# A recurrence of six steps: solved keys copied by two engines, keys turned before the second level's update

## The reference, cut to what matters

```python
kk = jnp.einsum('bhnid,bhnjd->bhnij', k, k)
t_mat = jnp.eye(c) + jnp.where(strict, kk * decay, 0.0) * beta[..., :, None]
u = solve(t_mat, v * beta[..., None])
wk = solve(t_mat, k * (beta * jnp.exp(gam))[..., None])
k_dec = k * jnp.exp(gam[..., -1:] - gam)[..., None]
# per chunk, in order:
w = u_c - jnp.einsum('bhck,bhkv->bhcv', wk_c, s)
s_new = cd_c * s + jnp.einsum('bhck,bhcv->bhkv', kd_c, w)
o = jnp.einsum('bhck,bhkv->bhcv', qd_c, s) + jnp.einsum('bhij,bhjv->bhiv', qk_c, w)
```

## Time and profile before

| what | us |
|---|---|
| median of 3 runs | 2874.38 (2871.8 to 2876.06) |
| profiled execution | 2869.82 |
| its span | 2868.0 |
| PE busy | 2716.9 (95%) |
| DVE busy | 1132.7 (39%) |
| ACT busy | 522.7 (18%) |
| POOL busy | 535.4 (19%) |
| mean granted TensorE clock | 0.975 |

### The profile page before, as it was taken

How to read it: one execution, slowest core, us unless ns; L and a number is a source line. 1 busy time by engine, 2 the same in 40 slices (tenths; PEclk the granted TensorE clock), 3 DMA queues, 4 the chain that set the end, 5 groups by cost and what they waited for, 6 DMA issues and landing times. The chain is left out here.

```text
span 2868.0 us, 35950 instructions
## 1 busy us (share of the span) xinstructions
PE 2716.9 (95%) x15102; PEld 1783.4 (62%) x15102; DVE 1132.7 (39%) x2206; ACT 522.7 (18%) x1160; POOL 535.4 (19%) x371
## 2 busy tenths in 40 slices
PE   7998999999999999999999999789969999996998
PEld 4443467777886446888887745788833337872333
DVE  2315633444412233444433265655232135643223
ACT  1324421000001232101001221444011011011011
POOL 1000002333341010244442300011000004431000
PEclk9999999999999999999999999999989999998999
DMA  8110115776222221222122301100279981228994
GB/s 261 72 68 34 44 58 218 270 264 214 82 94 86 88 85 45 78 85 88 66 81 118 111 16 60 39 17 10 117 306 421 421 352 69 84 99 350 421 421 202
DMA packets 70041, 431.11 MB, mean 150 GB/s; under 512 B 8202, under 2 KB 9017, under 8 KB 25720
## 3 DMA queue, kind: packets, MB, share of 16 engines
q1 hardware_dynamic: 65080, 412.48, 37.7%
q0 software_dynamic: 4800, 16.33, 1.6%
HBM read 422.33 MB, written 13.79 MB: 152 GB/s over the span
## 5 line engine op out<-in xcount | busy, mean ns | idle before, releaser
L461 PE MATMUL bank<-h,weight_ring 128*128 128x256 f32 x912 | 218.8, 383 | 1.1 <-DVE arena L385 1.0
L461 PEld LDWEIGHTS bank<-h,weight_ring 128*128 128x128 f32 x912 | 170.5, 190 | 36.9 <-issue 13.3
L1281 PE MATMUL bank<-h,weight_ring 128*128 128x512 f32 (+2 forms) x464 | 183.1, 547 | 5.4 <-DVE h L267 3.4
L3351 PE MATMUL bank<-h,weight_slots 128*128 128x256 f32 (+1 forms) x576 | 174.2, 459 | 0.0
L616 PE MATMUL bank<-arena,weight_ring 128*128 128x256 f32 x704 | 155.0, 379 | 0.0
L3351 PEld LDWEIGHTS bank<-h,weight_slots 128*128 128x128 f32 x576 | 109.7, 193 | 62.6 <-issue 46.8
L2835 PE MATMUL bank<-weight_slots,tokens_T 128*64 128x512 f32 x592 | 146.2, 613 | 1.3 <-issue 1.3
L1281 PEld LDWEIGHTS bank<-h,weight_ring 128*128 128x128 f32 (+1 forms) x464 | 86.8, 193 | 96.3 <-issue 87.7
L616 PEld LDWEIGHTS bank<-arena,weight_ring 128*128 128x128 f32 x704 | 133.7, 190 | 18.6 <-issue 0.4
L461 PE MATMUL bank<-h,arena 128*128 128x256 f32 x608 | 143.6, 379 | 0.0
L461 PEld LDWEIGHTS bank<-h,arena 128*128 128x128 f32 x608 | 115.5, 190 | 15.7
(11 more groups left out here) (549 smaller groups left out, 4482.5 us busy)
## 6 DMA issues: line engine op xcount, KB each, us to landing
arena<-in_ada_w SPq DMA_DIRECT2D x48, 1024.0 KB, 5.7
weight_ring<-in_gu SPq DMA_DIRECT2D x44, 1024.0 KB, 5.0
weight_slots<-in_w_up SPq DMA_DIRECT2D x42, 1024.0 KB, 26.0
weight_slots<-in_w_down SPq DMA_DIRECT2D x34, 1024.0 KB, 21.7
weight_slots<-in_w_gate SPq DMA_DIRECT2D x32, 1024.0 KB, 22.6
weight_ring<-in_w_gate SPq DMA_DIRECT2D x32, 1024.0 KB, 23.1
weight_ring<-in_w_down SPq DMA_DIRECT2D x30, 1024.0 KB, 23.7
weight_ring<-in_down SPq DMA_DIRECT2D x32, 704.0 KB, 4.1
```

Of the source, the lines that this page charges most:

```text
L461: m = pe.matmul(self.bank(q, i), weights[:, c * P:(c + 1) * P], tokens[:, c, :], start=(c == 0), stop=(c == 3))
L1281: m = pe.matmul(out, lhs, rhs, start=(c == 0), stop=(c == last - 1))
L3351: m = pe.matmul(self.bank(n)[:, 0:hi - lo], slot.buf[:, at:at + P], self.h[:, c, lo:hi], start=(c == 0), stop=(c == KT - 1))
```

## The change

Four edits, all in the recurrence.

1. The first half of the solved keys (bank 6) is still copied by ScalarE, as its first instruction, with a signal of its own; it no longer waits for the products with the state's second chunk (`ds`) and for the outputs (`o_done`), which are now waited for behind it. The second half (bank 7) is copied by VectorE in a new `keep_keys`, with a new signal `wk_kept`. `use_state` waits for both signals, `take_state` for the copies of w.
2. VectorE's `keep_keys` stands in front of `take_state` 0 in each step, and after the last solve behind the inversion of the head norm's factors.
3. In steps 1 and 2, level 0's product of direction 0 goes ahead of `use_state` 1.
4. The keys are turned after level 1's product of direction 0 and ahead of level 1's update of that direction, in all six steps; values are turned where they were.

```diff
-        self.uw_kept, self.grown_done = Turns(k.flag("delta_uw_kept"), n), each("grown_done", 2 * n)
+        self.uw_kept, self.grown_done = Turns(k.flag("delta_uw_kept"), 2 * n), each("grown_done", 2 * n)
+        self.wk_kept = Turns(k.flag("delta_scaled"), n)
...
         if i == 0:
-            after(pe, self.uw_kept, j)
+            after(pe, self.uw_kept, 2 * j)
+            after(pe, self.wk_kept, j)
...
+    def solved_keys(self, c):
+        return self.k.bank[:, 6 + c, :].rearrange("p (d h c) -> p d h c", d=2, h=DN_HEADS)
+
+    def keep_keys(self, v, j):
+        after(v, self.uw, j)
+        if j:
+            after(v, self.wk_s, 2 * j - 1)
+        v.tensor_copy(self.wk_T[:, 1, :, :, :], self.solved_keys(1)).then_inc(self.wk_kept.sem, 1)
+
     def keep_solved(self, a, j):
         after(a, self.uw, j)
         if j:
             after(a, self.wk_s, 2 * j - 1)
+        a.activation(self.wk_T[:, 0, :, :, :], self.solved_keys(0), ACT.Copy).then_inc(self.uw_kept.sem, 1)
+        if j:
             after(a, self.ds, 2 * j - 1)
         if j > LAT_FROM:
             after(a, self.o_done, 2 * (j - LAT_FROM) - 1)
-        for c in range(2):
-            a.activation(self.wk_T[:, c, :, :, :], self.k.bank[:, 6 + c, :].rearrange("p (d h c) -> p d h c", d=2, h=DN_HEADS), ACT.Copy)
         for i in range(2):
             last = a.activation(self.w[i][:, :, :], self.heads(4 + i, 0, P), ACT.Copy)
         last.then_inc(self.uw_kept.sem, 1)
...
     def take_state(self, v, j, i):
         after(v, self.wk_s, 2 * j + i)
-        after(v, self.uw_kept, j)
+        after(v, self.uw_kept, 2 * j + 1)
...
+                        if j <= LAT_FROM:
+                            c.level_z(pe, j, 0, 0)
                         c.use_state(pe, j - 1, 1)
-                        c.level_z(pe, j, 0, 0)
+                        if j > LAT_FROM:
+                            c.level_z(pe, j, 0, 0)
                         c.level_z(pe, j, 1, 0)
...
                     c.level_z(pe, j, 0, 1)
+                    for d in range(2):
+                        c.turn_keys(pe, j, d)
                     for n in range(1, LEVELS):
...
-                        if n < 3:
+                        if n == 2:
                             for d in range(2):
-                                (c.turn_keys if n == 1 else c.turn_values)(pe, j, d)
+                                c.turn_values(pe, j, d)
...
                     if j:
+                        c.keep_keys(v, j - 1)
                         c.take_state(v, j - 1, 0)
...
                 head.invert(v, MIDDLE)
+                c.keep_keys(v, LAST)
                 c.take_state(v, LAST, 0)
```

## The result

| | before | after |
|---|---|---|
| median of 5 runs | 2874.38 us (2871.69 to 2878.84) | 2859.70 us (2851.68 to 2860.90) |
| profiled execution (span) | 2869.82 (2868.00) | 2851.68 (2849.90) |
| recurrence, steps 0 to 5 | 219.98 | 203.69 |
| from the last solve to the last of the output stage | 79.35, clock 0.94 | 75.22, clock 1.00 |

The ratio is 0.9943 [0.9931, 0.9955]: 14.7 us less against 13.0 forecast, outside the 0.2% that counts as no change. The profiled pair differs by more, 18.1 us, because the changed kernel's profiled execution is the quickest of its five. The same kernel timed again beside the later experiments gave 2860.53 (2851.36 to 2866.32, 6 runs) against 2876.71, ratio 0.9941 [0.9925, 0.9957], 16.2 us. Single runs of it lie 15 us apart; where that comes from became half of this study.

The account below looks back on a forecast made before the run. TensorE, busy 95% of the span, was taken as the bound, starving in the recurrence steps. Copies 7.0, level-0 product 0.1, turns 3.95 and clock 1.9 summed to 13.0 us: median 2874.4 to 2861.4, range 2855 to 2869.

Parts of the forecast that it names:

- Copies, 5 × 1.35 + 0.24 = 7.0: After each solve, steps 1 to 5: TensorE starts 1.35 us sooner with two engines copying keys; 0.24 after the last.
- The bound of 0.9: Copies of solved keys: least gain per step, 0.9 us, if reading PSUM at once doubled ScalarE's 0.59 to 1.19.
- Rival three: After the solve: copies don't run side by side, or VectorE's take waits for copies of w; 2869.9 us, chance 0.09.
- The level-0 product, 0.1: Before the second use of the state: moving the product into TensorE's idle gains 0.1 us in step 1, nothing in 2.
- Turns in steps 1 and 2, 0.9 each: Level 1: idle ahead of the first update hides the key turns, the second update comes earlier; 0.9 us a step.
- Turns in steps 3 to 5, 0.55 each: Level 1: first update 0.35 us late behind the key turns, 0.90 saved at the second; net 0.55 a step.
- rival one: Level 1 turns: they only change place, leaving 1.4 us from clock and turns; 2865.9 us, chance 0.13.
- Step 0, 0.5: Turning keys ahead in step 0, at the low clock where turns take up to twice 1.02 us: gain 0.5.
- my bound of +1.0: Step 0's key turns: the most they were expected to gain, 1.0 us, with −1.0 as the lower bound.
- The clock, 1.9: TensorE's low-clock stretches: shorter idles win back 1.1 us in step 3 and 0.8 in step 2.
- rival two: Clock gives back more: steps 2, 3 and the last solve all at 2.4 GHz, 16.7 us; 2857.7, chance 0.12.
- Rival four, slower by the clock: Recurrence: low clock takes more of it, up to 20.1 us over steps 1 to 4; 2883.4 us, chance 0.04.

Follow-up runs that it names:

- The fill: The kernel before with only the two-engine copies, plus 4 idle matmuls in step 0 where the change has its turns; 2863.94 us, step 0 26.17.
- the changed kernel's second profile: The changed kernel, unedited, timed again beside later runs; median 2860.53 us against 2876.71 for the kernel before, ratio 0.9941.
- the copies alone: The changed kernel with keys turned in level 1 and level 0's product placed as before, keeping both engines' copies; median 2859.49 us, ratio 0.9958 to the kernel before.
- the turns alone: The kernel before with one edit, keys turned ahead of level 1's first update in all six steps; median 2869.25 us, ratio 0.9991.
- the unfilled version: The changed kernel with values turned earlier in steps 1 and 2, direction 0's query-key product earlier in steps 2 to 5, no idle matmuls; 2856.94 us, ratio 0.9940.
- one fill: The changed kernel with values and direction 0's masks earlier, plus five idle matmuls ahead of the last solve only; 2850.75 us, ratio 0.9927.
- fills at every solve: The changed kernel with values and masks earlier, plus idle matmuls: 8 ahead of step 0's level 0, 3 behind each solve, 5 ahead of the last; 2849.32 us, ratio 0.9905.

## Why the prediction was right, and where a size was off

- **Copies, 5 × 1.35 + 0.24 = 7.0.** TensorE waits 0.84 in place of 2.17 in each of the steps 1 to 5, 5 × 1.33, and the wait of 0.25 behind the last solve is gone: right. ScalarE's copy took 0.60 and VectorE's 0.69, the price of the earlier trace rows, while both read PSUM at once. The bound of 0.9 for slowed reading can be dropped: the Trainium skill (PSUM — Partial Sum Buffer, "Specifications (TRN2)") says that the two reach PSUM in parallel at full bandwidth as long as their banks don't collide, and the rows, with one bank for each, agree. Rival three is out; its mechanism lies 0.24 us away.
- **The level-0 product, 0.1.** 0.11.
- **Turns in steps 1 and 2, 0.9 each.** Step 1 gained 2.33 = 1.33 + 0.11 + 0.89: right. Updates follow each other after 2.15 (2.1 forecast).
- **Turns in steps 3 to 5, 0.55 each.** 1.79 − 1.33 = 0.46; the single runs give 0.36 to 0.56. The second update gained what was said, 0.9; the first came 0.42 late instead of 0.35. With 0.36 to 0.47 lost when the turns of steps 3 and 4 were put back, rival one (turns only change place) is out for the lengths of these steps.
- **Step 0, 0.5.** The mis-sized term: 1.96, outside my bound of +1.0. I had let the turns take twice their time at the low clock and stopped there. The fill showed that they also end that low clock earlier, 1.2 us, on top of their place, 0.8.
- **The clock, 1.9.** The mechanism was right, the number is none that one pair of profiles can give. The first pair showed 1.53 in step 2, 1.2 in step 3, about 1.7 in the last step and 3.9 in the output stage (4.13 less the 0.24 of the copies), 8.3 in all and beyond rival two; the changed kernel's second profile had step 2 at 0.91 and the output stage at 79.86 again, nothing won in either. The steady terms, copies 6.9, order 0.1, turns 3.2 and step 0's 1.96, make 12.2 us against 11.1 forecast (for steps 2, 3 and 5, which have no clean pair, the turns' share is taken from steps 1 and 4); the medians' 14.7 and 16.2 leave 2.5 to 4.0 for the clock. The halves show how little that is a property of an edit: the copies alone gained 5.5 more than their 7.1, the turns alone 2.4 less than their 5.2. That the output stage could gain at all was not in my sum: I had it full and so fixed, while it ran at 0.61 for its twelve microseconds from 2009.60 in the kernel before.
- **Rival four, slower by the clock.** Its mechanism showed in the turns alone, where step 1 at 0.86 took 36.94 against 33.4 (34.30 less the turns' 0.9). It took no more than one such step, and rival four needed more than two.

The prediction said that the trace agrees with the Trainium skill for step 3 as well. That was too much: the idle there was 2.17 us, shorter than the gaps that the page warns of, and only step 2's, 3.72, is of the kind that it means. The prediction's range, "from the bounds", was not their sum either: the lower bounds give 4.5 − 2.5 = 2 us, under the 5 that stood as its end.

So the forecast held, with step 0 sized 1.5 us too small and the clock 0.6 to 2.1. For the copies and the turns the mechanism was right. That the total came so near was in part luck, since the clock's 1.9 was counted on steps 2 and 3 and could as well have come out at nothing, as in the second profile, or at 8, as in the first. What stays open is what picks the execution in which the clock falls: the same order of instructions gave both outcomes.

## What to carry to other kernels

Where one engine makes several copies in a row and the next link needs only the first ones, put these first, under their own signal, and split them over the two engines that read PSUM; then measure how far the other copies are from being the next wait (here 0.24 us). Read a step's gain where the clock is 1.00 in both kernels, and treat the clock's part as a spread, not a sum: it also reaches into the stage behind, where TensorE is full. A few idle matmuls inside an idle may hold the clock, but only up to the length of that idle: 8 ahead of step 0, 3 behind each solve and 5 ahead of the last gained together, 8 behind each solve cost some 0.85 us a step.

## What the runs showed of the hardware that I had not expected

- TensorE's granted clock fell to its lower level (1.2 GHz) behind idles as short as 0.79 us in some executions (L2102 at 2.08), and stayed at 2.4 GHz behind 2.17 us in others. Once down it stayed there with TensorE busy for all of 12 us, at a mean of 0.57.
- The spread goes with the clock of the whole execution: the changed kernel's run of 2851.36 us had a mean of 0.979, the one of 2866.32 had 0.973. By my estimate 0.006 of 2860 us is 17 us of TensorE's time, enough for all 15. Not all of it lies in the recurrence and the stage behind: in the profiles with nothing filled ahead of it the recurrence itself starts anywhere from 1784.24 to 1791.18. Runs lay 6.4 us apart in the unfilled version, 5.2 with one fill and 1.8 with fills at every solve, five runs each.
- In step 0 the clock was up behind the kernel's fp32 transposes as it was behind matmuls (1.15 for L2008 behind either).
- An idle matmul in fp32 with a result of 64x128 costs 0.21 us at the full clock (eight in 1.67), so it can be dosed finely.
